# First attention: a pair's two maps are combined ahead of the turn and weighed one pair later; output products start between the last pair's softmax steps

## The reference

```python
def diff_attention(x, w_in, lam_p, subln_g, w_out, rel_bias, lam_init):
    ...                                     # H = 8 heads, two maps (m = 0, 1) of width 64 each
    s = einsum('bqhmd,bkhmd->bhmqk', q_blk, k) + bias
    s = where(rel >= 0, s, -inf)
    p = softmax(s, axis=-1)
    a = p[:, :, 0] - lam * p[:, :, 1]
    o = einsum('bhqk,bkhe->bqhe', a, v)     # v has 128 columns per head
    ...
    o = o * rsqrt(mean(o * o, axis=-1) + LN_EPS)
    o = o * subln_g * (1.0 - lam_init)
    return o.reshape(B, S, H * dv) @ w_out
```

## Time and profile before

| | us |
|---|---|
| median of 3 runs | 1439.22 (1438.13 to 1440.33) |
| profiled execution | 1439.74 |
| its span | 1437.6 |
| TensorE busy | 1301.8 (91%) |
| VectorE busy | 968.2 (67%) |
| ScalarE busy | 547.2 (38%) |
| POOL busy | 363.0 (25%) |

### The profile page before, as it was taken

How to read it: one execution, slowest core, us unless ns; L and a number is a source line. 1 busy time by engine, 2 the same in 40 slices (tenths; PEclk the granted TensorE clock), 3 DMA queues, 4 the chain that set the end, 5 groups by cost and what they waited for, 6 DMA issues and landing times.

```text
span 1437.6 us, 18188 instructions
## 1 busy us (share of the span) xinstructions
PE 1301.8 (91%) x5836; PEld 891.2 (62%) x5836; DVE 968.2 (67%) x2322; ACT 547.2 (38%) x1129; POOL 363.0 (25%) x378
## 2 busy tenths in 40 slices
PE   8999999999999999999899989768887989788877
PEld 6997888877988888877685734323343535343333
DVE  4687665565677556585864787777767677777755
ACT  4553544444664444454762222222222221222221
POOL 0104000000000000012503555444444444444540
PEclk9999999999999999999999999999999999999999
DMA  9714755645415555554423999999999999999997
GB/s 361 270 59 104 227 183 184 195 175 205 147 32 184 195 184 195 170 209 154 176 112 131 421 420 421 421 421 421 421 421 421 421 421 421 422 422 421 421 421 308
DMA packets 97538, 406.90 MB, mean 283 GB/s; under 512 B 6955, under 2 KB 44524, under 8 KB 60748
## 3 DMA queue, kind: packets, MB, share of 16 engines
q0 software_dynamic: 39552, 276.60, 46.9%
q1 hardware_dynamic: 57932, 129.60, 26.4%
HBM read 404.84 MB, written 1.07 MB: 282 GB/s over the span
## 4 chain that ended last, share of the span: by engine, by line
PE 56%; DMA 22%; DVE 9%; issue 8%; ACT 2%; POOL 2%; DVEq 0%; SPq 0%; POOLq 0%; ACTq 0%
DMA uv_proj<-in_peer_uv,prob 17%; PE ps_up L825 8%; PE ps L756 7%; PE ps L757 6%; PE ps L758 6%; PE ps L937 6%; PE ps_up L827 4%; DMA arena_u<-in_peer_uv,prob 3%; PE ps_up L756 3%; PE ps_up L758 3%; PE ps_up L757 3%; PE ps L1007 2%; DMA uv_mk<-in_peer_uv,prob 2%; PE ps_up L907 1%; POOL small L1851 1%
## 5 line engine op out<-in xcount | busy, mean ns | idle before, releaser
L2085 DVE TENSOR_TENSOR w_low<-ring,w_high 128x1024 fp32r<-128x1024 f32 x140 | 165.1, 1221 | 47.0 <-ACT w_high L1334 39.9
L825 PE MATMUL ps_up<-hT_both,w_high 128*128 128x512 f32 x512 | 182.0, 398 | 0.9 <-DVE hT_both L2078 0.9
L1334 ACT ACTIVATE w_high<-ring 128x1024 fp32r<-128x1024 f32 x140 | 140.4, 1052 | 69.8 <-PE ps L758 69.8
L937 PE MATMUL ps<-arena_u,sco 128*128 128x512 f32 x256 | 124.7, 632 | 33.5 <-ACT sco L1632 33.5
L937 PE MATMUL ps<-arena_v,sco 128*128 128x512 f32 x192 | 105.3, 678 | 50.3 <-ACT sco L1632 50.3
L827 PE MATMUL ps_up<-hT_both,w_low 128*128 128x256 f32 x512 | 143.7, 281 | 0.0
L1632 ACT ACTIVATE sco<-const,prob 128x128 f32<-128x128 f32 x256 | 84.7, 391 | 150.3 <-DVE prob L2785 128.9
L1644 ACT ACTIVATE prob<-prob 128x4 f32<-128x4 f32 (+2 forms) x67 | 13.8, 206 | 322.6 <-DVE prob L2775 322.6
L937 PE MATMUL ps<-ring,sco 128*128 128x512 f32 x256 | 116.5, 604 | 17.5 <-ACT sco L1632 17.5
L1857 POOL TENSOR_SCALAR small<-small 128x1 f32<-128x1 f32 x8 | 4.3, 534 | 491.8 <-ACT arena_v L1366 491.8
L2775 DVE CUSTOM_DVE_ANT_0 arena_u<-arena_u,nat 128x1024 f32<-128x1024 f32 x64 | 78.1, 1225 | 67.7 <-DMA arena_u<-in_peer_uv,prob 67.6
(11 more groups left out here) (496 smaller groups left out, 2866.1 us busy)
## 6 DMA issues: line engine op xcount, KB each, us to landing
ring<-in_w_up SPq DMA_DIRECT2D x32, 1024.0 KB, 5.5
ring<-in_w_down SPq DMA_DIRECT2D x32, 1024.0 KB, 4.9
qkring<-in_qk_a SPq DMA_DIRECT2D x8, 1024.0 KB, 5.6
qkring<-in_qk_b SPq DMA_DIRECT2D x8, 1024.0 KB, 4.9
ring<-in_w_in SPq DMA_DIRECT2D x8, 860.0 KB, 4.8
arena_v<-in_peer_wq SPq DMA_DIRECT2D x5, 1024.0 KB, 9.0
ring<-in_w_out_a SPq DMA_DIRECT2D x4, 1024.0 KB, 14.9
ring<-in_v_b SPq DMA_DIRECT2D x4, 1024.0 KB, 5.8
```

The lines of the kernel that those rows point to most:

```text
L825: pe.matmul(ps_up[:, 2 * b + fb, :].rearrange("p (a s) -> p a s", a=2), high, hT_both[:, :, c, :], start=(c == 0), stop=False, skip_group_ ...
L937: last = pe.matmul(ps[2 * t + n][:, :], diag[:, k % N_DIAG, :], slots[k][:, D + n * HALF:D + (n + 1) * HALF], start=(first and k == 0), st ...
L1334: sc.activation(w_split[pair][0][:, part], ring[:, slot, part], ACT.Copy)\
L2085: ve.tensor_tensor(w_split[pair][1][:, part], ring[:, slot, part], w_split[pair][0][:, part].bitcast(F32), ALU.subtract)\
```

## The change

1. The two maps of a pair are combined before they are turned. The softmax is left unnormalised: VectorE makes `prob0 + prob1 * (-lam * total0 / total1)` in place (`mix`). The common factor `1/total0` is left out, and the epsilon of the root mean square is multiplied by `total0` squared (`eps_in`) instead. One map of three tiles is turned (`turn_mix`), copied by ScalarE (`take_mix`), and weighed by three products (`weigh_mix`).
2. TensorE's order for a pair is now: scores, both projections of the next pair, turns of pair f, weighing of pair f-1. The weighed result is copied out of its bank by ScalarE (`take_weighed` into `mixed`); VectorE takes squares and the output scale of pair f-2 around the combination of pair f.
3. The end is rewritten. Before the scores of pair 7 the first column pair of `nat` is turned; `out_pair(0)` runs ahead of the turns of pair 7, and pair 7 is weighed within `out_pair(1)`. The last column pair is turned in the middle of `last_out_pairs`, behind four product groups instead of ahead of them. Banks and the order of splits on ScalarE and VectorE follow.
4. One semaphore is saved (`turned_s` serves for the bias rows).

The diff, cut to its core, with eight columns of indentation taken off:

```diff
@@ -250,9 +250,11 @@
...
+mixed = tmp[:, 1, 512:D].rearrange("p (b t d) -> p b t d", b=2, t=NT)
...
+eps_in = piece(4).rearrange("p (b t) -> p b t", b=2)
...
@@ -659,32 +661,57 @@
...
+    def turn_mix(b, bank=None):
+        pe.wait_ge(sem("probs_final"), count.take("probs_final"))
+        bank = 2 + b if bank is None else bank
+        for k in range(3):
+            last = pe.transpose(ps[bank][:, k * P:(k + 1) * P], prob[:, b, 0, k * P:(k + 1) * P], ident)
+        last.then_inc(sem("probT_a_turned"), 1)
+    def weigh_mix(b, v):
+        pe.wait_ge(sem("probT_a"), count.take("probT_a"))
+        o = ps[6 + b]
+        pe.matmul(o[:, 0:P], probT[:, b, 0:P], v(0), start=True, stop=True)
+        pe.matmul(o[:, P:2 * P], probT[:, b, P:2 * P], v(0), start=True, stop=False)
+        pe.matmul(o[:, P:2 * P], probT[:, b, 2 * P:3 * P], v(1), start=False, stop=True)\
+            .then_inc(sem("weighed"), 1)
+    def mix_block(f, b, first=False):
+        pair_scores(b, (0, 1))
+        project(1 - b, 0, reverse=True)
+        project(1 - b, 1)
+        turn_mix(b)
+        if not first:
+            weigh_mix(1 - b, lambda t: val[:, t, bass.ds((f - 1) * P, P)])
+    def mixed_attention_layer():
         values()
         project(0, 0, reverse=True)
         project(0, 1)
         pe.wait_ge(sem("val_v"), count.take("val_v", 2))
         pe.wait_ge(sem("val_a"), count.take("val_a", 2))
-        with count.loop(3, qk_split0=2, qk_split1=2, qkT_ready=4, probs_ready=8, probT_v=2, probT_a=2) as i:
-            for b in range(2):
-                attend_block(i * 2 + b, b, dv)
-        attend_block(6, 0, dv)
-        attend_block(7, 1, dv, more=False)
+        mix_block(0, 0, first=True)
+        with count.loop(3, qk_split0=2, qk_split1=2, qkT_ready=4, probs_final=2, probT_a=2) as i:
+            for n in range(2):
+                mix_block(i * 2 + (1 + n), 1 - n)
+        pe.wait_ge(sem("nat_ready"), count.take("nat_ready"))
+        turn_pair(0, 3)
+        pair_scores(1, (4, 5))
+        weigh_mix(0, lambda t: val[:, t, 6 * P:7 * P])
+        turn_pair(1, 7)
+        pe.wait_ge(sem("hT_split"), count.take("hT_split"))
+        out_pair(0)
+        turn_mix(1, 4)
+        pe.wait_ge(sem("nat_ready"), count.take("nat_ready"))
+        turn_pair(2, 5)
+        pe.wait_ge(sem("hT_split"), count.take("hT_split"))
+        out_pair(1, lambda: weigh_mix(1, lambda t: val[:, t, 7 * P:8 * P]))
+        last_out_pairs(turned=False)
+        count.skip("probs_ready", 32)
...
         pe.wait_ge(sem("hT_split"), count.take("hT_split"))
-        if not turned:
-            pe.wait_ge(sem("nat_ready"), count.take("nat_ready"))
-            turn_pair(3, 6)
         for cc in range(2):
             take_half(2, cc, (turn[0] + 2) % 4)
             for k in (0, 1):
                 out_part(2, cc, k)
+        if not turned:
+            pe.wait_ge(sem("nat_ready"), count.take("nat_ready"))
+            turn_pair(3, 6)
         for k in (2, 3):
             out_part(2, 0, k)
...
@@ -1279,10 +1297,9 @@
...
-    pe.matmul(ps[3][0:HEADS, 0:384], relb_sb, bucket_sb, start=True, stop=True).then_inc(sem("bias_rows_ready"), 1)
-    attention_layer(P)
+    pe.matmul(ps[3][0:HEADS, 0:384], relb_sb, bucket_sb, start=True, stop=True).then_inc(sem("turned_s"), 1)
+    mixed_attention_layer()
     landed("pe_table")
-    split_natural()
...
-            dst, src = hT_high[:, 2 * c:2 * c + 2, :], ps[(4, 5, 4, 6)[c] if reverse else 4 + c][:, :]
+            dst, src = hT_high[:, 2 * c:2 * c + 2, :], ps[(3, 7, 5, 6)[c] if reverse else 4 + c][:, :]
...
@@ -1438,24 +1455,57 @@
...
+    def take_mix(b, bank=None):
+        sc.wait_ge(sem("probT_a_turned"), count.take("probT_a_turned"))
+        sc.activation(probT[:, b, :], ps[2 + b if bank is None else bank][:, 0:384], ACT.Copy)\
+            .then_inc(sem("probT_a"), 1)
+    def take_weighed(b):
+        sc.wait_ge(sem("weighed"), count.take("weighed"))
+        sc.activation(mixed[:, b, :, :], ps[6 + b][:, 0:S].rearrange("p (t d) -> p t d", t=NT), ACT.Copy)                    .then_inc(sem("mix_taken"), 1)
+    def mix_block(b, first=False):
         exps(b)
...
+        take_projection(1 - b, 0)
+        qk_high(b, 0)
+        take_projection(1 - b, 1)
+        qk_high(b, 1)
+        take_mix(b)
+        if not first:
+            take_weighed(1 - b)
+    def mix_blocks():
+        mix_block(0, first=True)
+        mix_block(1)
+        with count.loop(2, sco_ready=8, proj_ready=4, probT_a_turned=2, weighed=2, qk0_landed=16, qk1_landed=16):
+            mix_block(0)
+            mix_block(1)
+        exps(0)
+        take_projection(1, 0)
+        sc.wait_ge(sem("qk_split1"), count.take("qk_split1", 8))
+        split_high(0, 1)
+        take_projection(1, 1)
+        take_weighed(1)
+        take_mix(0)
+        take_turned_high(reverse=True, pairs=(0,))
+        take_weighed(0)
+        exps(1)
+        take_turned_high(reverse=True, pairs=(1,))
+        split_high(1, 3)
+        split_high(2, 2, halves=(0,))
+        take_mix(1, 4)
+        take_turned_high(reverse=True, pairs=(2,))
+        split_high(2, 2, halves=(1,))
+        take_weighed(1)
...
     def out_and_mlp(turned=False):
-        if not turned:
-            take_turned_high(reverse=True, pairs=(2,))
-        split_high(2, 2)
         if turned:
...
-            bank = (4, 5, 4, 6)[c] if reverse else 4 + c
+            bank = (3, 7, 5, 6)[c] if reverse else 4 + c
...
@@ -2127,42 +2160,69 @@
...
+    def mix(b):
         ve.wait_ge(sem("probs_ready"), count.take("probs_ready", 4))
-        then(ve.reciprocal(share[:, b, :, :], total[:, b, :, :]))
-        then(ve.tensor_scalar(share[:, b, 1, :], share[:, b, 1, :], lam_exp[:, 2:3], None, ALU.mult))
-        ve.wait_ge(sem("weighed"), count.take("weighed"))
+        ve.scalar_tensor_tensor(out=eps_in[:, b, :], in0=total[:, b, 0, :], scalar=LN_EPS, in1=total[:, b, 0, :],
+                                op0=ALU.mult, op1=ALU.mult)
+        then(ve.reciprocal(share[:, b, 1, :], total[:, b, 1, :]))
+        then(ve.scalar_tensor_tensor(out=share[:, b, 0, :], in0=share[:, b, 1, :], scalar=lam_exp[:, 2:3],
+                                     in1=total[:, b, 0, :], op0=ALU.mult, op1=ALU.mult))
+        for t, (a, z) in enumerate(((0, P), (P, 384))):
+            last = ve.scalar_tensor_tensor(out=prob[:, b, 0, a:z], in0=prob[:, b, 1, a:z],
+                                           scalar=share[:, b, 0, t:t + 1], in1=prob[:, b, 0, a:z], op0=ALU.mult,
+                                           op1=ALU.add)
+        then(last)
+        ve.sem_inc(sem("probs_final"), 1)
+    def mix_squares(b):
+        ve.wait_ge(sem("mix_taken"), count.take("mix_taken"))
         for t in range(NT):
...
+            last = ve.tensor_tensor_reduce(tmp[:, 1, t * P:(t + 1) * P], mixed[:, b, t, :], mixed[:, b, t, :],
+                                           1.0, 0.0, ALU.mult, ALU.add, sq_sum[:, t:t + 1])
+        then(last)
+        then(ve.scalar_tensor_tensor(out=ms_in[:, 0:2], in0=sq_sum[:, 0:2], scalar=1.0 / P, in1=eps_in[:, b, :],
+                                     op0=ALU.mult, op1=ALU.add))
+        ve.sem_inc(sem("ms_ready"), 1)
+    def mix_out(f, b):
         ve.wait_ge(sem("rms_ready"), count.take("rms_ready"))
         for t in range(NT):
-            last = ve.scalar_tensor_tensor(out=nat[:, t, bass.ds(f * P, P)], in0=omap[:, t, :],
+            last = ve.scalar_tensor_tensor(out=nat[:, t, bass.ds(f * P, P)], in0=mixed[:, b, t, :],
                                            scalar=ms_out[:, t:t + 1], in1=subln, op0=ALU.mult, op1=ALU.mult)
         then(last)
...
+    def mix_blocks():
+        for f in range(8):
+            b = f % 2
+            if 1 <= f < 7:
+                qk_low(1 - b, 1)
+            add_rel_bias(b, f, (4, 5) if f == 7 else (0, 1))
+            if f > 1:
+                mix_squares(b)
+            mix(b)
+            if f > 1:
+                mix_out(f - 2, b)
+            if f < 6:
+                qk_low(b, 0)
+            else:
+                ve.sem_inc(sem("nat_ready"), 1)
+            if f == 6:
+                split_low(0, 1)
+                take_turned_low(hT_low_qkv, reverse=True, pairs=(0,))
+        take_turned_low(hT_low_qkv, reverse=True, pairs=(1,))
+        split_low(1, 3)
+        mix_squares(0)
+        mix_out(6, 0)
+        take_turned_low(hT_low_qkv, reverse=True, pairs=(2,))
+        ve.wait_ge(sem("weighed"), count.take("weighed", 8))
+        split_low(2, 2, halves=(0,))
+        mix_squares(1)
+        split_low(2, 2, halves=(1,))
+        mix_out(7, 1)
...
         if s == 0:
-            take_turned_low(hT_low_qkv, reverse=True, pairs=(2,))
-        split_low(2, 2)
-        if s == 0:
             take_turned_low(hT_low_qkv, reverse=True, pairs=(3,))
         else:
```

More of the change, by code:

```diff
@@ L768, in out_part @@
                 return last
[L770 to L777, removed]
             def out_pair(j, between=lambda: None):
@@ L1457, in attention_layer @@
```

(48 more changed lines are left out.)

46 lines of the change are left out of this document (8 added, 38 removed).

## The result

The changed kernel takes 1428.84 us (median of 4 runs, 1428.16 to 1429.43), the kernel before 1439.6 beside it: ratio 0.9926, 95% interval 0.9914 to 0.9938. That is 10.8 us less; forecast were 1429.4 us and 9.8 us less. A second measurement of both on another occasion gave 1428.86 and 0.9931 (0.9917 to 0.9944).

The account below looks back on a forecast made before the run. TensorE was taken to bound the loop over pairs, a VectorE and ScalarE chain the last pair. Savings of 7.1 us (loop) and 2.7 us (tail) make 9.8, taking 1439.22 to 1429.4 us; range 1427.4 to 1432.4.

Parts of the forecast that it names:

- Scores and two projections: TensorE's loop over pairs: scores and both projections take 6.66 us per pair, as in the second attention.
- Three turns: TensorE's loop: three turns behind the projections take 0.42 us per pair, 0.75 less three at 0.11.
- Weighing: TensorE's loop: six weighing passes at 0.11 us plus 0.1 for the change to the scores take 0.76 us.
- Loop: First attention's seven pairs on TensorE: 54.36 us against 61.42, saving 7.1 us.
- What hides: VectorE's work beside each pair: combined map ready 5.25 us after scores, wanted at 6.66, so 1.4 us to spare.
- Rival C: Loop: combined map late on every pair; kernel slower from 2.8 us delay per pair, 1442 us at 3.2; chance 0.03.
- Products start at T+2.7: Tail: output products start 2.7 us after T, the first pair turn, against 8.85 us after the last scores before.
- New wait 1.5: Tail: TensorE newly waits 1.5 us behind the last pair turn for the split of `w1`; bounds 0 and 3.4.
- rival A: Tail: the new wait halves TensorE's clock, losing 1.7 us, giving 1431.1 us; chance 0.16.
- Layer norm 0.26 late: After the output products: VectorE's first residual starts late, and all but 0.26 us is caught up when products end.
- Gain goes through whole: Behind the stage: nothing changes and later stages wait for its `h`, so all 9.8 us reach the total.
- rival D: Feed-forward: its first weights don't come earlier with the stage's 9.8 us, so no change, 1439 us; chance 0.03.

Follow-up runs that it names:

- the delayed kernels: Changed kernel with three or six scratch additions on VectorE ahead of every combination: 1432.37 us with three, 1444.25 us with six.
- the six additions: Changed kernel with six scratch additions (2.7 us per pair) on VectorE ahead of every combination: 1444.25 us.
- first filled kernel: Changed kernel with 15 identity turns put into TensorE's 1.81 us wait at the start of the third block: 1426.44 us.
- the one with the moves: Changed kernel with that wait filled by 15 turns, `w1` split ahead of the last turned pair, and that pair turned behind two product groups: 1425.63 us.

## Why the prediction was right

- **Scores and two projections, 6.66:** 6.67 (66.03 to 72.70). Reading the second attention for the new order was the step that made the sum close.
- **Three turns, 0.42:** 0.33. This is the term that was mis-sized. I took 0.75 less three turns and so kept 0.1 of a change-over that rows 3 show and this loop doesn't; six turns in this loop take 0.65. Over seven pairs it is 0.6 us.
- **Weighing, 0.76:** 0.76 (73.03 to 73.79), and 0.65 for six passes when doubled. The 0.11 us of the rows held against the Trainium skill's 81 ns (page "TensorE: Matmul & The Clock Gate", section "Back-to-back issue gap"); the trace does not agree with that figure for these fp32 passes.
- **Loop, 54.36:** 53.75 (43.22 to 96.97), saved 7.7 instead of 7.1.
- **What hides:** the map was ready at 5.1 (said 5.25). But "1.4 us to spare" named the wrong resource. By the delayed kernels VectorE's round is the next bound, with 1.1 us of room, and the thin margins of the tail are used up before the map is late. Rival C's point, 2.8 us of delay, was therefore too far: at 2.7 the kernel was 5 us slower than before (1444.25 against 1439.31). An estimate: on a line between the stages with 1.35 and 2.7 us of delay (92.5 and 103.8), the 100.3 of before is met at about 2.3.
- **Products start at T+2.7:** 2.52. **End at T+28.7:** 28.65 (125.62 less 96.97).
- **New wait 1.5:** 1.59, released by the split of `w1`, and removed by changing only the order of that split. The clock stayed at 1.00 behind it, here and in the eight other executions that had this wait, so rival A did not happen.
- **Layer norm 0.26 late:** nothing. From the products' end to the feed-forward's start it is 7.19 us (125.62 to 132.81), 7.18 before. VectorE started the residuals at 121.63, 0.4 us earlier than I had it, and so caught up.
- **Gain goes through whole:** yes, 1294.6 against 1294.3 us behind the stage. That rules out rival D. Some luck was in it: both executions had the fall of the clock at the start of the third block. Had only one of them had it, the difference would have been off by 1.5 us, and the prediction did not reckon with that.

The sum: 0.6 from the turns, 0.26 from the layer norm and 0.05 in the tail make the 0.9 us between the 9.8 forecast and the 10.7 in the trace.

The split of the gain between the parts depends on the order in which they are taken. Against before the tail gave 3.0 us; starting the products late again costs 7.2, more than the whole tail gained, since late products fare worse with the new splits and copies around them: 43.0 us from the first pair turn to the feed-forward (97.06 to 140.09) against 38.9 from the last scores in before (104.42 to 143.31), and 3.4 of the 43.0 are the clock. The loop without its lag is worth nothing. The opposite kernel, with the lag but both maps turned and weighed, was not run, so how much the lag alone would gain is not shown.

## What to carry to other kernels

If the same kernel already has a stage in the order that a change introduces, take the step times from there, but take each term between starts of the same two kinds of instruction. For "how much room is there" follow the whole round of the helping engine, and sort its idle time: the 0.41 us ahead of ScalarE's exponentials, which wait for VectorE's own peaks, moved along with the delay and couldn't be spent, while the 1.09 us ahead of the key split, whose pace TensorE set, could. Cutting work on the bounding engine pays only if its next input is there: lag the consumer by a step first. When a fix gains more than the stage it touches, cut both traces at fixed landmarks before crediting it.

## What the runs showed of the hardware that I had not expected

The length of a wait on TensorE does not by itself decide whether the clock falls. Behind 1.59 us (at 118 us) it stayed at 1.00 in every kernel that had the wait; behind 1.69 us and two shorter ones it fell; behind 1.47 to 1.58 us in each pair, six times in a row, it stayed at 1.00; behind the 1.75 us of the row below it never fell in fourteen executions, nor behind 1.72 to 1.77 us at another place near 320 us; behind the 1.92 us of the six additions it fell, and behind 3.24 us it was 0.51 for 7 us; and behind one and the same wait of 1.81 us, with the same work ahead of it, it fell to half in seven of twelve profiled executions and stayed in five; in one of the five it fell at 684 us instead. Each fall behind that wait cost about 1.5 us. TensorE's timeline, changed kernel:

```profile
663.69 0.63 PE L1153 MATMUL ps<-const,proj 128*128 128x128 f32 x4 [1.75 <-ACT proj L1730]
```

The traces show what goes with the one or the other. In each execution all changes of the granted clock, hundreds of microseconds apart, lie on one evenly spaced series of instants, to within 0.002 us. Carried on to the wait of 1.81 us, an instant came between 0.06 us ahead of its end and 1.45 us behind it in each of the seven executions in which the clock fell. In none of the five in which it stayed did one come there: the next behind the end came at 1.58 to 2.58 us. So where the wait lies in that series, which any shift of the work ahead moves, separates all twelve. No run set this position on purpose, so it is a match in twelve executions and not a tested cause. It also makes the fill's effect surer: in the first filled kernel the instant lay 0.13 us behind the wait's end, among those with a fall, and the clock stayed. In the one with the moves it lay 0.20 us ahead of the end, outside both groups.

For a change worth 1 to 2 us this is as large as the effect, and the first scores, too, started between 41.6 and 43.7 us in kernels that don't differ ahead of them, so the stage's length in the trace was a better measure than the median.
